# Attention: the pieces of the loop over sample pairs in another order on TensorE, VectorE and ScalarE

## The reference

```python
def nsa_sample(a, pool_cmp, pool_sel, buf_win, page_table, w_in, w_cmp, q_gain, k_gain, w_out, rel_bias):
    q, kv_c, kv_s, kv_w, gates = nsa_project(a, w_in, q_gain)
    ...
    o_c, imp = cmp_branch(q, compress(rows_c, w_cmp), q_pos, rel_bias, k_gain[0])
    imp_sel = ...                       # importance of each block of 64 past rows
    o_s = sel_branch_sample(q, kv_s, pool_sel, page_table, imp_sel, past_len, rel_bias, k_gain[1])
    o_w, new_buf = win_branch_sample(q, kv_w, buf_win, past_len, rel_bias, k_gain[2])
    y = nsa_merge(gates, o_c, o_s, o_w, w_out)

def sel_branch_sample(...):
    _, idx = lax.top_k(score, n_top)    # 15 blocks; the first and the last are forced
    ...
    return sel_attend(q, rmsnorm(rows[..., 0, :], k_gain), rows[..., 1, :], k_pos, q_pos, rel_bias)
```

## Time and profile before

| | us |
|---|---|
| median of three runs | 1261.41 |
| lowest and highest | 1257.84, 1264.43 |
| profiled execution | 1262.4 |
| its span | 1260.7 |
| TensorE busy in the span | 1189.1 |
| VectorE, ScalarE, GpSimd busy | 471.2, 280.3, 221.3 |
| first selected_keys of pair 0 | 590.19 |
| first selected_keys of pairs 1, 2, 3 | 627.23, 670.89, 714.81 |
| window_values(3), just behind the loop | 757.84 |

### The profile page before, as it was taken

The page is one execution under the profiler, slowest core; times in us unless marked ns, Lnnn a source line. Parts: engine busy times, 40 slices in busy tenths (PEclk is TensorE's granted clock), DMA queues, the critical chain, the costliest instruction groups (busy, mean ns, idle before and its releaser), DMA issues.

```text
span 1260.7 us, 36543 instructions
## 1 busy us (share of the span) xinstructions
PE 1189.1 (94%) x14710; PEld 983.7 (78%) x14710; DVE 471.2 (37%) x1368; ACT 280.3 (22%) x749; POOL 221.3 (18%) x376
## 2 busy tenths in 40 slices
PE   8999999999999998999678869989999999999998
PEld 6887877999999976873355547787887978978976
DVE  2111116677774322004676763433211311312223
ACT  1000003100010021335877852210010110110121
POOL 4133232012340000413445440000000000000000
PEclk9999999999999998999998979999999999999999
DMA  9998899998334264645587686599999999999831
GB/s 327 311 310 289 288 303 284 226 354 288 130 139 181 94 277 167 157 105 164 152 276 214 225 256 237 150 410 378 404 354 356 356 367 386 356 354 376 313 121 37
DMA packets 122955, 329.99 MB, mean 262 GB/s; under 512 B 17864, under 2 KB 56729, under 8 KB 121124
## 3 DMA queue, kind: packets, MB, share of 16 engines
q1 hardware_dynamic: 96628, 259.88, 57.0%
q0 software_dynamic: 16656, 59.30, 16.1%
q10 hardware_dynamic: 9504, 8.48, 2.3%
HBM read 319.16 MB, written 15.70 MB: 266 GB/s over the span
## 4 chain that ended last, share of the span: by engine, by line
PE 82%; DVE 5%; issue 4%; DMA 3%; SPq 2%; ACT 2%; POOLq 0%; POOL 0%; DVEq 0%; ACTq 0%
PE bank L2006 17%; PE bank L2644 15%; PE bank L2113 12%; PE pbank L2655 6%; PE bank L2149 6%; PE pbank L2644 3%; PE bank L2655 3%; PE bank L2064 3%; PE bank L2217 2%; SPq L611 1%; SPq L621 1%; DMA gring<-in_moe 1%; PE bank L2596 1%; PE bank L2288 1%; DMA gring<-in_conv_in 1%
## 5 line engine op out<-in xcount | busy, mean ns | idle before, releaser
L2644 PE MATMUL bank<-X,gring 128*64 128x96 f32 x4608 | 196.5, 246 | 4.5 <-issue 4.2
L2644 PEld LDWEIGHTS bank<-X,gring 128*64 128x64 f32 x4608 | 192.2, 137 | 9.3 <-issue 9.3
L2006 PE MATMUL bank<-aT,gring 128*128 128x288 f32 x768 | 193.6, 411 | 6.1 <-DVE aT L1337 3.5
L2006 PEld LDWEIGHTS bank<-aT,gring 128*128 128x128 f32 x768 | 146.7, 192 | 49.0 <-issue 5.3
L2655 PE MATMUL pbank<-Q,X 128*32 128x256 f32 x1152 | 80.8, 379 | 0.8 <-issue 0.8
L621 POOL DMA_DIRECT2D Q<-in_cache_cmp x96 | 51.8, 539 | 123.0 <-issue 123.0
L2113 PE MATMUL bank<-aT,gring 128*128 128x144 f32 x528 | 72.3, 286 | 0.3 <-issue 0.3
L2113 PEld LDWEIGHTS bank<-aT,gring 128*128 128x128 f32 x528 | 67.8, 190 | 0.5 <-issue 0.5
L1932 DVE TENSOR_TENSOR X<-X,bank 128x96 f32<-128x96 f32 x72 | 18.4, 255 | 133.1 <-ACT X L1282 132.6
L1925 DVE TENSOR_TENSOR hT<-hT,bank 128x288 f32<-128x288 f32 x48 | 18.8, 447 | 130.6 <-PE bank L2596 130.6
L2006 PE MATMUL bank<-Q,gring 128*128 128x288 f32 x256 | 63.3, 407 | 1.6 <-DMA gring<-in_conv_out 1.5
(11 more groups left out here) (390 smaller groups left out, 1789.1 us busy)
## 6 DMA issues: line engine op xcount, KB each, us to landing
gring<-in_moe SPq DMA_DIRECT2D x176, 512.0 KB, 5.9
Q<-in_moe SPq DMA_DIRECT2D x72, 512.0 KB, 7.9
gring<-in_dense_gu SPq DMA_DIRECT2D x44, 512.0 KB, 13.2
gring<-in_conv_in SPq DMA_DIRECT2D x24, 512.0 KB, 8.1
Q<-in_cache_cmp POOLq DMA_DIRECT2D x96, 128.0 KB, 4.1
Q<-in_cache_cmp SPq DMA_DIRECT2D x96, 128.0 KB, 4.0
gring<-in_dense_down SPq DMA_DIRECT2D x16, 704.0 KB, 5.4
Q<-in_cache_cmp ACTq DMA_DIRECT2D x64, 128.0 KB, 3.7
```

The costliest lines, as they stand in the source:

```text
L2006: ins = pe.matmul(bank(label, k)[:, 0:T], tile[:, 128 * i:128 * i + 128], rhs[:, i, :], start=i == 0, stop=i == C - 1)
L2644: ins = pe.matmul(m_bank(i, M_GU + f)[64 * w:64 * w + 64, CAP * u:CAP * u + CAP], gslot(("m", 0), 2 * f + u)[:, o:o + 64], ae[:, c, :], st ...
```

## The change

In the loop body of each of the three engines the same pieces are called in another order; `prompt_steps()` and `result_order()` number their buffers in the new order. Each piece and each wait in it is the same, and GpSimd's and SyncE's rows and the order of the ring are the same. Lines of the changed kernel are 14 (ScalarE), 20 (VectorE) and 15 (TensorE) higher. The loop bodies, cut to the moved parts:

```diff
@@ TensorE
                 selected_keys(p, 1)
-                prompt_logits(2 * p, 1)
                 if p:
                     selected_values(p - 1, 0)
+                transposes(p, 0)
+                if p:
+                    prompt_transposes(2 * p - 1, 0)
                     selected_values(p - 1, 1)
-                    prompt_transposes(2 * p - 1, 0)
-                transposes(p, 0)
+                prompt_logits(2 * p, 1)
                 transposes(p, 1)
-
+                if p < 3:
+                    compressed_logits(p + 1)
                 if p:
                     prompt_transposes(2 * p - 1, 1)
                 selected_keys(p, 2)
                 if p:
-                    selected_values(p - 1, 2)
                     prompt_values(2 * p - 1)
-                if p < 3:
-                    compressed_logits(p + 1)
-
                 prompt_logits(2 * p + 1, 0)
                 selected_keys(p, 3)
                 if p:
+                    selected_values(p - 1, 2)
                     selected_values(p - 1, 3)
...
+                transposes(p, 6)
+                transposes(p, 3)
+                if p < 3:
                     importance(p + 1)
-
+                transposes(p, 2)
                 prompt_transposes(2 * p, 0)
+                transposes(p, 5)
+                transposes(p, 4)
                 if p:
                     values_transposed(p - 1)
-                transposes(p, 6)
-                transposes(p, 2)
-                transposes(p, 3)
                 prompt_transposes(2 * p, 1)
-                transposes(p, 4)
-                transposes(p, 5)
                 prompt_values(2 * p)
@@ VectorE
                 if p:
                     prompt_scale(2 * p - 1)
-
+                    prompt_transposed(2 * p - 1, 0)
                 selected_scores(p, 1)
                 prompt_scores(2 * p, 1)
                 if p:
                     selected_values(p - 1, 0)
+                    prompt_transposed(2 * p - 1, 1)
                     selected_values(p - 1, 1)
-                    prompt_transposed(2 * p - 1, 0)
...
                 prompt_transposed(2 * p, 0)
+                prompt_transposed(2 * p, 1)
                 if p < 3:
                     blocks_chosen(p + 1)
-                prompt_transposed(2 * p, 1)
+                prompt_out(2 * p)
                 if p:
                     sample_out(p - 1)
-                prompt_out(2 * p)
@@ ScalarE
                 key_scale(p, 1)
+                if p:
+                    prompt_exps(2 * p - 1, 1)
                 key_squares(p, 4)
                 key_squares(p, 5)
-                if p:
-                    prompt_exps(2 * p - 1, 1)
...
+                key_squares(p, 8)
                 key_scale(p, 3)
-                key_squares(p, 8)
                 key_squares(p, 9)
-                prompt_exps(2 * p, 1)
...
```

More of the change, by code:

```diff
@@ L94, in prompt_steps @@
 def prompt_steps():
-    o = [(0, L0), (0, L1)]
-    for k in range(1, 8):
-        o += [(k, L0), (k, L1), (k - 1, T0), (k - 1, T1)]
+    o = []
+    for p in range(4):
+        o += [(2 * p, L0)]
+        o += [(2 * p - 1, T0)] if p else []
+        o += [(2 * p, L1)]
+        o += [(2 * p - 1, T1)] if p else []
+        o += [(2 * p + 1, L0), (2 * p + 1, L1), (2 * p, T0), (2 * p, T1)]
     o += [(7, T0), (7, T1)]
@@ L1228, in _ @@
                 exps(1, SN[p % 2], smt[:, 4:5], sexp_ready)
-                for t in range(4):
-                    exps(1, S[:, 512 * t:512 * t + 512], smt[:, t:t + 1], sexp_ready)
+                exps(1, S[:, 0:512], smt[:, 0:1], sexp_ready)
                 if p < 3:
                     key_scale(p + 1, 0)
+                exps(1, S[:, 512:1024], smt[:, 1:2], sexp_ready)
+                transposed(p, 6)
+                exps(1, S[:, 1024:1536], smt[:, 2:3], sexp_ready)
+                if p < 3:
+                    key_squares(p + 1, 2)
+                exps(1, S[:, 1536:2048], smt[:, 3:4], sexp_ready)
+                transposed(p, 5)
+                if p < 3:
+                    key_squares(p + 1, 3)
+                transposed(p, 3)
+                if p < 3:
                     importance(p + 1)
+                transposed(p, 4)
+                transposed(p, 2)
+                if p < 3:
                     window_exps(p + 1)
-                    key_squares(p + 1, 2)
-                    key_squares(p + 1, 3)
-                for i in (6, 2, 3, 4, 5):
-                    transposed(p, i)
                 prompt_exps(2 * p + 1, 0)
@@ L1808, in _ @@
                     selected_values(p - 1, 0)
+                    prompt_transposed(2 * p - 1, 1)
                     selected_values(p - 1, 1)
-                    prompt_transposed(2 * p - 1, 0)
+                if p < 3:
+                    compressed_scores(p + 1)
                 window_factor(p)
-                if p:
-                    prompt_transposed(2 * p - 1, 1)
                 selected_scores(p, 2)
+                prompt_scores(2 * p + 1, 0)
+                if p < 3:
+                    compressed_probabilities(p + 1)
                 if p:
@@ L1826, in _ @@
                     selected_values(p - 1, 3)
-                if p < 3:
-                    compressed_probabilities(p + 1)
                 prompt_scores(2 * p + 1, 1)
```

38 lines of the change are left out of this document (24 added, 14 removed).

## The result

The changed kernel takes 1250.39 us (median of 15 runs, 1242.33 to 1254.15) against 1260.93 us for the kernel before beside it: a ratio of 0.9911, 95% interval 0.989 to 0.9931, so 10.5 us or 0.9% faster.

What follows compares the result with a forecast made beforehand. The loop was taken as bound by the path from GpSimd's first issue through the landing of sk(p, 3, 1) and the tail. With periods of 42.7 us it ends 7.2 sooner: 1261.41 - 7.2 = 1254.2 us, range 1247.5 to 1262.0.

Steps and rivals of the forecast that it cites:

- F(p): First GpSimd issue of iteration p after its mask; forecast at 629.4 for pair 1 and 714.8 for pair 3.
- L: Time from the last issue of page set sk(p, 3, 1) to its landing; taken as 6.0 us, bounds 3.0 and 6.3.
- The front at nothing: Front: removing TensorE's 2.99 us stops takes 9.0 us off its idle time, but nothing was booked directly for it.
- The tail: From selected_scores(p, 3) to the next selected_keys: 16.4 us become 14.6, 1.8 shorter; in pair 3, 14.2 become 12.4.
- The period: One loop iteration: 12.84 + L 6.0 + 4.6 + 14.6 + 4.64 = 42.7 us, against 44.05 and 43.54.
- GpSimd's limit: GpSimd's 32 issues, mask and next issue: one cycle can't be shorter than 41.4 us.
- the rival with short landings: Landings of 3.0 us make GpSimd's 41.4 the period: loop end 12.8 sooner, 1248.6 us; chance 0.20.
- The price of the late mask: The next mask waits for blocks_chosen, so the first issue follows selected_keys(p+1, 0) by 4.04 + 0.6 instead of 3.2.
- The slower rival: Late blocks_chosen delays each mask and page set by 1.3, prompt_exps adds 1.9: 6.9 us slower, 1268.3; chance 0.10.
- Contention: Mask beside selected_scores(p+1, 0) slows one VectorE step from 0.75 to 1.52: 0.8 a pair, kept for the range.
- The clock: Fronts: without the 2.99 us stop TensorE stays at full clock, each front saving up to 1.8 us more.
- One for one to the end: Behind the loop: a shift of window_values(3), from 757.84 to 750.6, passes unchanged to the kernel's end.

Runs made afterwards that it cites:

- sync_loads: Changed kernel with the tiles sk(p, 3, 1) of pairs 1 to 3 loaded by SyncE instead of GpSimd; ratio 0.9978 against the kernel before.
- keys_first: Changed kernel with GpSimd issuing the pages of sk(p, 3, 1) ahead of those of sv(p-1, 2, 1) in pairs 1 to 3; ratio 0.9956 against the kernel before.
- after_again: The changed kernel unaltered, run and profiled a second time beside the experiments; 1247.47 us, ratio 0.9882 against the kernel before.
- new_tail_only: Kernel before with the new tail order alone, front and middle in the old order; ratio 0.9935 against the kernel before.
- keys_logits: keys_first with prompt_logits, window_keys, prompt_scores and prompt_scale moved ahead of the late selected_values work on TensorE and VectorE; 1248.72 us, ratio 0.9885.
- choice_late: Kernel before with only blocks_chosen moved behind prompt_transposed(2p, 1) on VectorE; ratio 1.004 against the kernel before.
- after: The changed kernel in its first series and profiled execution; 1250.39 us, ratio 0.9911 against the kernel before.
- choice_first: Changed kernel with blocks_chosen put back ahead of prompt_transposed(2p, 1) on VectorE, nothing else; 1264.13 us, ratio 1.0026 against the kernel before.
- vector_tail: Kernel before with VectorE's tail in the new order, values_transposed moved to suit the banks, ScalarE unchanged; ratio 0.9954 against the kernel before.

## Why the prediction was right, and where its sizes were off

**What bounds the loop: right, for the profiled execution.** The way from F(p) to square 9 through the landing was the gate in all three pairs, and L was 6.28, 6.21 and 5.97 us where 6.0 was taken (644.43 less the last issue at 638.15, and so on). sync_loads and keys_first show it from the other side: the head of pair 1 fell to 25.4 and 25.6 when that load came sooner. But L is not a constant. In after_again square 9 of pairs 1 and 2 started 4.2 and 4.6 us behind the last issue of its set without a wait, so L was no more than that, and it was 5.3 in pair 3; the head of pair 1 was 25.4 there too, with the loads as they were. So some 25.4 us is what the engines need in the new order, and in the profiled execution the landing added up to 1.6. What makes a landing late in one execution and not in the next stays open.

**The front at nothing: right in the profiled execution, not settled beyond it.** new_tail_only keeps the 9.0 us of stops, and its loop is 2.0 us longer, of which pair 0 makes 1.3. With landings as in after_again the new front would be worth more, and the timed series put it at 3 to 7 us. The exponentials ahead of the squares were covered, as booked: selected_scores(1, 1) came 2.3 us later behind selected_keys(1, 0) than before, and selected_scores(1, 2) 0.5 sooner.

**The tail: right in kind, too small.** 1.8 us a pair was forecast for pairs 1 and 2, and 2.3 and 2.0 came; 0.95 and 0.3 were booked in pair 0, where head and tail gave 2.5, because the move of blocks_chosen helps there too. I had let pair 0 count through F(1) alone. Its gain there was 1.0 by the forecast; counted from the loop's start F(1) fell from 40.2 to 38.5, by 1.7. In pair 3 it was 1.4 against 1.8.

**The period: mis-sized, and GpSimd's limit too high.** The sum had 42.7 us, and 41.07 and 41.38 came (626.14, 667.21, 708.59). The terms, forecast and measured: last issue of the page set 12.84 and 12.0; L 6.0 and 6.2; to selected_scores(p, 3) 4.6 and 4.7; tail 14.6 and 14.1 to 14.4; mask and next issue 4.64 and 4.0. Two steps failed. The 0.6 us pause does not exist behind a mask, where the issue follows at once. And 12.84 was read in a row of issues that each had a pause, while behind the mask the first ones come closer. The loop gained 11.6 us and not 7.2. Of the missing 4.4, F(1) makes 0.7, the two periods 3.0, most of it these two terms, and the way from F(3) to the end 0.7. For the same reasons GpSimd's cycle can be shorter than the 41.4 us that the prediction called its least: without their idle time the periods are 40.7 and 39.8 us here, and 39.15 in keys_logits. The period that came is close to that of the rival with short landings, for another reason: its landings of 3.0 us did not come.

**The price of the late mask: right.** F follows selected_keys(p, 0) by 4.0 instead of 3.2 to 3.6. GpSimd stood idle for the choice ahead of each mask; 0.39 and 1.61 us of that, in pairs 2 and 3, are new. The slower rival did not happen; choice_late shows that its mechanism was near, with sample_out and not the mask as what came late.

**Contention: not paid.** By the rule quoted from the Trainium skill (SBUF — State Buffer, section Who interferes with whom) 0.8 us a pair was kept for the range. The mask of pair 2 ended at 667.27, and the step of selected_scores(2, 0) that had taken 1.52 started at 667.49 and took 0.75. In pairs 1 and 3 it started 0.24 us behind the mask's end and took 0.75 too: the two don't meet in the new order, so the rule had nothing to act on. In pair 0, where they meet as before, it took 1.52 again.

**The clock: half right.** The loop's granted clock was 0.96 to 1.00 where it had been 0.84 to 0.92 in pairs 1 to 3. The Trainium skill (TensorE: Matmul & The Clock Gate, section HAM oscillation — how this bites in real kernels) states that a loop rearranged so that TensorE does not wait in it again and again stays warm. The trace agrees in the profiled execution, not in after_again, and new_tail_only has the stops and the full clock in two fronts of three. What the half clock cost before is 2.6 us in the head of pair 3, which the sum had inside its landing term; pair 1's head was held by the landing anyway. Which idle stretch brings the clock down, and why not each time, stays open.

**One for one to the end: not shown.** The prediction let a shift of the loop's end pass to the end of the kernel unchanged. The stretch behind the loop took 502.9 us before and 498.7 and 504.6 after, and it holds a wait for in_ple_proj that was 0, 1.1, 3.9 and 6.7 us in after, after_again, keys_logits and sync_loads, and 3.7 in choice_first, whose loop is the longest. With one or two traced executions of a kernel, what sets this wait stays open.

## What to carry to other kernels

Between engines with a fixed order, what stands behind a piece counts more than how long an engine idles: ask of each piece who waits for whatever is queued behind it, and by which buffer. Move pieces in the sets that share such a buffer; one of them alone can cost more than all together bring. And once the engines are ordered, sum up the path from a DMA's issue to its use around the loop: it decides how much of an engine's gain arrives, and a load that comes sooner only helps if the next one does. Look behind the loop too, and at a second trace before you settle on what the gate is.

## What the runs showed of the hardware that was not expected

A stop of 2.99 us on TensorE was followed by half clock in some places and not in others of the same kernel: selected_keys(p, 2) took 1.94 us behind it in pair 2 of vector_tail and 1.06 in pair 3 of the same execution, and the granted clock was 1.00 in pair 3 of new_tail_only. GpSimd's issues are 1.14 us apart in a row (0.54 of its own and 0.60 of pause), but the first two behind a mask took 1.09 us together, without a pause. And the stretch behind the loop, the same instructions each time, took from 498.7 to 513.5 us in the profiled executions, a spread wider than the whole change is worth; without the timed series beside the traces the whole time would have told little.
